# Two decoder layers on one core: expert stages regrouped, and the routing chain ahead of them rearranged

## What is computed

```
g_prob = softmax(xf @ wg + bg);  g_idx = argmax(g_prob)
e_sel  = (xf @ we + be) of the 8 experts of that group
top_v, top_i = top_k(e_sel, 2)                 # two experts per token
weights = g_w * softmax(top_v)
h = silu(xs @ w_gate[e]) * (xs @ w_up[e])      # 1024 -> 512, twice
y = (h @ w_down[e]) * weights                  # 512 -> 1024
x = x + sum of a token's two results
```

## Time and profile before

| | |
|---|---|
| median of 3 runs | 2049.12 us (2048.31 to 2049.97) |
| the profiled execution | 2047.72 us, its span 2046.0 us |
| PE busy | 1912.6 us, 93% of the span |
| DVE, ACT, POOL busy | 779.7, 536.8, 98.4 us |
| read from HBM | 486.44 MB |
| PE L976 (gate and up), L991 (down) | 22% and 11% of the chain that ended last |
| PE L946 (gathers), L968 (mixes) | 6% each of that chain |

### The profile page before, as it was taken

How to read it: one execution, slowest core, us unless ns; L and a number is a source line. 1 busy time by engine, 2 the same in 40 slices (tenths; PEclk the granted TensorE clock), 3 DMA queues, 4 the chain that set the end, 5 groups by cost and what they waited for, 6 DMA issues and landing times.

```text
span 2046.0 us, 22955 instructions
## 1 busy us (share of the span) xinstructions
PE 1912.6 (93%) x9568; PEld 1214.2 (59%) x9568; DVE 779.7 (38%) x1144; ACT 536.8 (26%) x968; POOL 98.4 (5%) x122
## 2 busy tenths in 40 slices
PE   6999999897999999999799969989879999999997
PEld 5875778674444444443588869967664444444443
DVE  4466564535222223222433363455352232222222
ACT  3416352533111111110244332334341111111110
POOL 2200010000000000000100050000000000000000
PEclk8999999998999999999899989989989999999999
DMA  6220342134999999999424302323127999999996
GB/s 228 83 67 16 104 144 83 42 101 177 405 408 406 409 405 410 407 404 415 165 93 144 99 12 96 105 102 103 37 90 299 411 406 407 405 412 410 402 410 258
DMA packets 99930, 490.09 MB, mean 240 GB/s; under 512 B 7760, under 2 KB 16016, under 8 KB 50544
## 3 DMA queue, kind: packets, MB, share of 16 engines
q1 hardware_dynamic: 96928, 478.18, 59.7%
q0 software_dynamic: 2320, 8.29, 1.2%
q10 hardware_dynamic: 576, 2.10, 0.3%
HBM read 486.44 MB, written 2.10 MB: 239 GB/s over the span
## 4 chain that ended last, share of the span: by engine, by line
PE 84%; DVE 6%; ACT 5%; issue 3%; POOL 1%; DMA 0%; DVEq 0%; ACTq 0%; POOLq 0%
PE ps L623 25%; PE ps L976 22%; PE ps L991 11%; PE ps L946 6%; PE ps L968 6%; PE ps L620 6%; PE ps L903 1%; PE ps L790 1%; PE ps L884 1%; ACT hT L1485 1%; DVE wl L510 1%; PE ps L636 1%; ACT wh L501 1%; DVE nat L1620 1%; DVE xnl L2105 1%
## 5 line engine op out<-in xcount | busy, mean ns | idle before, releaser
L976 PE MATMUL ps<-ring,xg 128*64 128x512 f32 x1536 | 346.3, 596 | 2.8 <-issue 2.5
L510 DVE TENSOR_TENSOR wl<-ring,wh 128x512 fp32r<-128x512 f32 x280 | 192.0, 695 | 388.4 <-ACT wh L501 387.4
L501 ACT ACTIVATE wh<-ring 128x512 fp32r<-128x512 f32 x280 | 174.2, 629 | 428.4 <-PE ps L623 350.7
L2097 DVE TENSOR_TENSOR x<-ps,x 128x1024 f32<-128x1024 f32 x128 | 150.6, 1219 | 334.7 <-PE ps L968 334.7
L623 PE MATMUL ps<-wh,ah 128*128 128x512 f32 x544 | 217.7, 400 | 7.5 <-DVE wl L510 3.1
L976 PEld LDWEIGHTS ps<-ring,xg 128*64 128x64 f32 x1536 | 105.2, 137 | 201.2 <-issue 196.9
L623 PE MATMUL ps<-wl,ah 128*128 128x512 f32 x544 | 214.9, 395 | 0.0
L623 PE MATMUL ps<-wh,al 128*128 128x512 f32 x544 | 214.8, 395 | 0.0
L991 PE MATMUL ps<-ring,hT 128*64 128x512 f32 x768 | 173.6, 601 | 4.7 <-ACT hT L1485 1.4
L1509 ACT ACTIVATE xg<-ps,grow 128x256 f32<-128x256 f32 x128 | 53.4, 470 | 350.0 <-PE ps L946 327.7
L2093 DVE TENSOR_TENSOR yl<-ps,yh 128x1024 fp32r<-128x1024 f32 x32 | 39.2, 1224 | 234.4 <-ACT yh L1488 234.4
(11 more groups left out here) (300 smaller groups left out, 2601.4 us busy)
## 6 DMA issues: line engine op xcount, KB each, us to landing
ring<-in_moe_w_gate SPq DMA_DIRECT2D x96, 1024.0 KB, 9.2
ring<-in_moe_w_up SPq DMA_DIRECT2D x96, 1024.0 KB, 8.3
ring<-in_moe_w_down SPq DMA_DIRECT2D x96, 1024.0 KB, 8.4
slot<-in_moe_w_up SPq DMA_DIRECT2D x32, 1024.0 KB, 8.8
slot<-in_moe_w_gate SPq DMA_DIRECT2D x32, 1024.0 KB, 9.2
slot<-in_moe_w_down SPq DMA_DIRECT2D x32, 1024.0 KB, 9.0
ring<-in_x_wkv SPq DMA_DIRECT2D x16, 1024.0 KB, 5.1
ring<-in_c_w_in SPq DMA_DIRECT2D x16, 1024.0 KB, 5.2
```

The source lines that it names most:

```text
L501: act.activation(wh[:, t % STAGE, :], ring[:, unit % RING, 512 * s:512 * (s + 1)], ACT.Copy).then_inc(wh_ready, 1)
L510: dve.tensor_tensor(wl[:, t % STAGE, :], ring[:, unit % RING, 512 * s:512 * (s + 1)], wh[:, t % STAGE, :].bitcast(F32), ALU.subtract).then ...
L976: mm = pe.matmul(ps[p * SLOTS:(p + 1) * SLOTS, bank, :], xg[:, b % 2, k, r * P + p * SLOTS:r * P + (p + 1) * SLOTS], w(p)[:, k % 4, :], st ...
L2097: return dve.tensor_tensor(x[:, m, :], ps[:, bank:bank + 2, :].rearrange("p a n -> p (a n)"), x[:, m, :], ALU.add)
```

## The change

Pair q on PE becomes: gate 0, gate 1, up 0, up 1; gather; mixes 0 and 1 of pair q-1; gather; mixes 2 and 3; hidden transposes, slot weights, slot transposes; down 0, down 1. With the next pair's gate and up that makes six weight stages in a row. The slot transposes move to bank 5. DVE forms the hidden rows ahead of the four adds; results are split in two halves of 512 columns by ACT and DVE. Ahead of the experts, the token split is done in halves of the columns: the first half beside the last dense product, the second behind `lgT`; two transposes are placed ahead of a product; `all_taken` moves behind the first gate stage; `most_slots` goes ahead of the second `oh`; and matmuls whose results nobody reads run where PE would wait (17 ahead of the ranks, 7 ahead of the first gathers).

```diff
-GATE, UP, TURN, Y, GATHER, MIX, SEL = 0, 1, 2, 3, 5, 6, 6
+GATE, UP, TURN, Y, GATHER, MIX, SEL = 0, 1, 2, 3, 5, 6, 5
...
+            def idle_products(bank, n):
+
+                for _ in range(n):
+                    pe.matmul(ps[:, bank, :].rearrange("p (a n) -> p a n", n=P), identr[:, :],
+                              identr[:, :].unsqueeze(1).to_broadcast([P, TM, P]), start=True, stop=True)
...
                 products(0, 0, (0, 4))
-                products(0, 1, (0, 4))
                 for m in range(3):
                     x_turn(l, 1, m)
+                products(0, 1, (0, 4))
...
                 b = begin(("rank", l, 0))
+                idle_products(b + 2, 17)
                 pe.wait_ge(S["cnt_ready"], l + 1)
...
                     if bank == GATHER:
                         after(pe, S["xg_ready"], 4 * (b0 + b) + block)
+                        if b and block % 2 == 0:
+                            pe.wait_ge(S["selT_ready"], q0 + 2 * b + block // 2 - 1)
...
                 def first_gathers():
 
+                    idle_products(GATHER, 7)
                     pe.wait_ge(S["oh_ready"], b0 + 1)
...
                 def do_mix(q, m, bank):
                     if m == 0:
-                        pe.wait_ge(S["y_split"], q0 + q + 1)
-                        pe.wait_ge(S["selT_ready"], q0 + min(q + 2, PAIRS))
-                    if m >= 2:
-                        pe.wait_ge(S["y_added"], 4 * (q0 + q) + m - 1)
-                    mix(q, m, bank).then_inc(S["mixed"], 1)
...
+                        pe.wait_ge(S["selT_ready"], q0 + q + 1)
+                        after(pe, S["y_added"], 4 * (q0 + q))
+                        for half in range(2):
+                            pe.wait_ge(S["y_split"], 2 * (q0 + q) + half + 1)
+                            mm = mix_half(q, 0, bank, half)
+                    else:
+                        if m >= 2:
+                            pe.wait_ge(S["y_added"], 4 * (q0 + q) + m - 1)
+                        mm = mix(q, m, bank)
+                    mm.then_inc(S["mixed"], 1)
...
                     do_hidden(q, GATE, 0)
-                    if q:
-                        do_mix(q - 1, 0, MIX)
-                        do_mix(q - 1, 1, Y)
-                    else:
+                    if q == 0:
+                        all_taken(pe, ("nmix", l + 1, 0))
                         do_gather(0, 3, Y + 1)
...
                     do_hidden(q, UP, 0)
-                    if q:
-                        do_mix(q - 1, 2, MIX)
-                        do_mix(q - 1, 3, Y)
...
                         do_gather(b + 1, 2 * (q % 2), GATHER)
+                    if q:
+                        do_mix(q - 1, 0, MIX)
+                        do_mix(q - 1, 1, Y)
+                    if more:
+                        do_gather(b + 1, 2 * (q % 2) + 1, GATHER)
+                    if q:
+                        do_mix(q - 1, 2, MIX)
+                        do_mix(q - 1, 3, Y)
                     pe.wait_ge(S["h_ready"], q0 + q + 1)
...
                     do_down(q, 1)
-                    if more:
-                        do_gather(b + 1, 2 * (q % 2) + 1, GATHER)
...
                 for m in range(TM):
-                    high(1, m)
+                    xn_high(0, m)
+                for m in range(3):
+                    high(1, m)
+                square(1, 0)
+                high(1, 3)
+                for m in range(1, TM):
                     square(1, m)
...
-                xn_his((0, 1))
                 b = round_done(act, ("route", l, 0)) + 3
                 act.activation(lgT[:, :], ps[0:2 * ROUTES, b, :], ACT.Copy).then_inc(took(("route", l, 0)), 1)
-                xn_his((2, 3))
+                for m in range(TM):
+                    xn_high(1, m)
...
                 def pair(q):
...
+                    hide(q)
                     if q:
                         for m in range(TM):
                             do_add(q - 1, m, Y if m % 2 else MIX)
...
                 columns(0)
-                for m in range(1, TM):
-                    xn_lo(l, m)
+                for m in range(TM):
+                    xn_lo(l, 1, m)
                 slot_table(l)
+                most_slots(l)
                 columns(1)
-                most_slots(l)
```

More of the change, by code:

```diff
@@ L962, in slots_T, with mix_half @@
                 return mm
+            def mix_half(q, m, bank, half):
+                for i, a in enumerate((yh, yl)):
+                    mm = pe.matmul(ps[:, bank + half, :], selT[:, q % 2, m * P:(m + 1) * P],
+                                   a[:, 512 * half:512 * (half + 1)], start=(i == 0), stop=(i == 1))
+                return mm
             def mix(q, m, bank):
                 for half in range(2):
-                    for i, a in enumerate((yh, yl)):
-                        mm = pe.matmul(ps[:, bank + half, :], selT[:, q % 2, m * P:(m + 1) * P],
-                                       a[:, 512 * half:512 * (half + 1)], start=(i == 0), stop=(i == 1))
+                    mm = mix_half(q, m, bank, half)
                 return mm
@@ L1123, in experts @@
                 pair(PAIRS - 1)
[L1124 to L1127, removed]
+                do_mix(PAIRS - 1, 0, MIX)
+                do_mix(PAIRS - 1, 1, Y)
+                do_mix(PAIRS - 1, 2, MIX)
+                do_mix(PAIRS - 1, 3, Y)
                 pe.wait_ge(S["y_added"], TM * PAIRS * (l + 1))
@@ L1488, in results_hi, with result_hi @@
                 return act.activation(yh[:, :], ps[:, Y:Y + 2, :].rearrange("p a n -> p (a n)"), ACT.Copy)
+            def result_hi(half):
+                return act.activation(yh[:, 512 * half:512 * (half + 1)], ps[:, Y + half, :], ACT.Copy)
             def experts(l):
                 q0, b0 = PAIRS * l, BATCHES * l
-                def xn_his(tiles):
-                    for m in tiles:
-                        act.activation(as_row(xnh[:, m, :]), by_row(x[:, m, :]), ACT.Copy).then_inc(S["xn_hi"], 1)
-                xn_his((0, 1))
                 b = round_done(act, ("route", l, 0)) + 3
                 act.activation(lgT[:, :], ps[0:2 * ROUTES, b, :], ACT.Copy).then_inc(took(("route", l, 0)), 1)
-                xn_his((2, 3))
+                for m in range(TM):
+                    xn_high(1, m)
                 act.wait_ge(S["g_sub"], l + 1)
@@ L1527, in pair @@
                         gathered(b + 1, 2 * (q % 2), GATHER)
+                        gathered(b + 1, 2 * (q % 2) + 1, GATHER)
                     act.wait_ge(S["hT_done"], q0 + q + 1)
@@ L1532, in pair @@
                     after(act, S["mixed"], 4 * (q0 + q))
-                    results_hi().then_inc(S["yh_ready"], 1)
-                    if more:
-                        gathered(b + 1, 2 * (q % 2) + 1, GATHER)
+                    for half in range(2):
+                        result_hi(half).then_inc(S["yh_ready"], 1)
                 gathered(0, 0, GATHER)
@@ L1974, in cross @@
                     low(0, m)
+                for m in range(2):
+                    xn_lo(l, 0, m)
                 b = round_done(dve, ("xo", l, 1))
@@ L2094, in results_lo, with result_lo @@
                                          ALU.subtract)
+            def result_lo(half):
+                part = slice(512 * half, 512 * (half + 1))
+                return dve.tensor_tensor(yl[:, part], ps[:, Y + half, :], yh[:, part].bitcast(F32), ALU.subtract)
             def add(m, bank):
@@ L2098, in add, with xn_lo @@
                                          ALU.add)
[L2100 to L2105, removed]
+            def xn_lo(l, c, m):
+                n = 2 * TM * l + TM * c + m
+                dve.wait_ge(S["xn_hi"], n + 1)
+                dve.tensor_tensor(half_row(xnl[:, m, :], c), half_by_row(x[:, m, :], c), half_row(xnh[:, m, :], c).bitcast(F32),
                                   ALU.subtract).then_inc(S["xn_lo"], 1)
@@ L2165, in experts @@
                 pair(PAIRS - 1)
-                for m, bank in enumerate((MIX, Y, GATE, MIX)):
-                    do_add(PAIRS - 1, m, bank)
+                for m in range(TM):
+                    do_add(PAIRS - 1, m, Y if m % 2 else MIX)
                 with dve.If(n > SLOTS):
@@ L2204, in _ @@
                 cross(l)
-                xn_lo(l, 0)
+                for m in range(2, TM):
+                    xn_lo(l, 0, m)
                 route(l)
```

38 lines of the change are left out of this document (20 added, 18 removed).

## The result

The changed kernel takes 2030.17 us (median of 4 runs, 2024.31 to 2031.18) against 2049.55 for the kernel before (4 runs beside it). The ratio is 0.9899, 95% interval 0.9878 to 0.9919: faster by 1.0%. I had predicted 2010, and 2000 to 2026. The sign was right, the size about twice too large, and the time lies outside the range. The profiled execution took 2031.18 us, its span is 2029.4.

A forecast was written before the change was run, and what follows sets the result against it. PE was taken to set the 30.95 us period, with loads close behind. Per layer 6.3 - 0.5 + 10.4 + 2.0 + 0.7 = 18.9 us, twice 37.8, off 2047.72 gave 2009.9, predicted as 2010; range 2000 to 2026.

The forecast's parts named there:

- What bounded the kernel before: Experts' pairs: PE sets the 30.95 us period, with the load limit only 0.8 to 1.5 us below.
- The steady pair on PE: Steady expert pairs: six stages 20.73 plus a group of 9.42 give 30.15 us, 0.80 less, 10.4 us a layer.
- The loads: Expert weight loads: engines keep up at 418 GB/s or more; up 1 lands at about 16, needed at 17.2.
- the loads set it: Rival, steady pairs: loads below 418 GB/s set the period, 9 to 20 us less gain, 2019 to 2029; chance 0.20.
- The last pairs: Pairs 14 and 15, without gathers: 26.9 us each, gains of 1.1 and 0.9, together 2.0 a layer.
- Pair 0: First pair of a layer, without mixes: some 0.5 us longer, as its second gather waits for ACT's copy.
- Ahead of the experts: Routing to first expert stage: 3.0 from earlier logits, 2.1 from DVE's halves, 1.2 from PE's wait; 6.3 us a layer.
- The clock: Rival, ahead of the experts: half clock delays the gathers, 2.5 us a layer lost, 2015; chance 0.08.
- The ends of the layers: Layer's end: halved results start the mixes 0.9 earlier, the four adds lengthen by 0.2; 0.7 us gained.
- Slower: Rival, steady pairs: up 1 starves, slower when its landing takes over 11.8 us; 53 us slower at 13.8; chance 0.03.
- adds hidden: Rival, steady pairs: mixes and adds overlap better, loads bind at 29.6 to 29.9 us, 1996 to 2004; chance 0.10.
- does nothing: Rival, steady pairs: broken runs cost the same inside a group, the period stays, only the ends gain, 2031; chance 0.01.

The follow-up runs named there:

- e2: Kernel before the change, with the experts' weight loads cut to 14% fewer bytes: 2048.99 us, ratio 1.0002.
- e3: Changed kernel with the low half of every mix left out, 1.8 us less PE work a pair, loads unchanged: 2014.94 us.
- e1: Changed kernel with the experts' weight loads cut to 14% fewer bytes: 2009.95 us, ratio 0.9814 to the kernel before.
- e8: Changed kernel with 33 unread products ahead of the ranks in place of 17, and 5 ahead of the gathers in place of 7: 2029.87 us.
- e10: Kernel before with only the part of the change ahead of the experts, its pairs left as they were: 2037.85 us, ratio 0.9955.
- e12: Changed kernel with mixes 0 and 1 between gate 1 and up 0, and 33 and 5 unread products for 17 and 7: 2023.94 us, ratio 0.9879.

## Why the prediction was wrong, point by point

By the two profiled executions 16.5 us were gained in place of 37.8. The missing 21.3 are 7.3 in the thirteen periods of each layer, 8.3 from the fifteenth pair's first stage to the last down stage's end, 1.1 in pair 0, 2.5 ahead of the experts and 4.0 outside the change, less 1.9 more than forecast at the ends.

**What bounded the kernel before:** right. e2 shows that PE alone set 30.95.

**The steady pair on PE:** right, 30.09 for 30.15. The adds end last, by 0.29 us. This step alone would have given 0.86 a period.

**The loads: the step that failed.** I had asked whether the mean rate sufficed (418 GB/s) and whether up 1's load, "there at about 16", came before 17.2. It came at 17.4 in the pair shown (559.52 - 542.13), 10.3 after its permission, with a use that stands 10.3 after it. The room was even less than that: PE starts 0.14 behind the landing, and a stage behind a wait takes 3.65 in place of 3.43, so a landing later than about 9.9 costs. My 16, that is 9.1 after the permission, had been worked out from a mean rate, as if all of a load arrived at once. In the steady pairs the load's first steps came at 8.3 to 8.9 and its last at 9.6 to 11.2, and wherever the last was later than 9.9 the period was that landing plus 20.15.

```profile
547.10:559.50 12.40, 12.40 (x58) 4.65 (x54) 1.29 (x2) 1.77 (x3) 0.00 (x0) 1.00 0.98 400
```

The engines were not idle meanwhile: between 547.1 and 559.5 they moved 400 x 12.4 = 4.96 MB, of which the four up loads are 4.19. The queue had not run dry either, as I had thought it nearly would: when up 0's loads were issued (545.82), two gate loads were still to land, the second from 547.47 to 549.34. From the steps' times I estimate that some 0.3 MB of the other 0.8 belonged to this load, ahead in the queue, and some 0.5 MB to the down loads behind, moved while the last share of up 1 lagged. The cost in the steady pairs was 9.2 us of stretch, 7.5 us against the forecast.

The rival "the loads set it" had the right cause, and said 2019 to 2029 at 0.20. It had the wrong rule: loads that always queue reach 420 (e3), and what binds is the distance of 10.3 us against the landing of a load's last share. And I ended the range at 2026, inside it.

**The last pairs: a second failure of the same step.** I took PE's 26.9 for both, and in e1 they are nearly that (26.95 to 27.6). But a pair's loads take 30.0, so without gathers PE outruns them. The last two intervals, down 0 to down 0, were 27.7 and 29.8 in the first layer, 27.0 and 31.1 in the second, where before they were 30.1 and 27.7. Against e1 that is 7.1 us for both layers, and against 26.9 each time it is 7.9. It needed no measurement: 26.9 stood beside 29.9 in the prediction.

**Pair 0:** 1.0 us a layer longer, from the first stage to the next pair's, where I had allowed 0.5.

**Ahead of the experts:** 4.8 and 5.3 us in place of 6.3. The logits came 3.0 earlier, as forecast (from the routing's start to L2034 9.3, before 12.3), DVE's halves took 4.13 (4.4 forecast), and PE no longer stood before the first stage for DVE. The clock took 1.0 to 1.6 back; I had named that, but set it at nothing in the sum. Where it held, in e8, the way was 25.8, that is 6.4 and 6.2 less than before: the rest of this step was right.

**The ends of the layers:** 0.6 for the first, 0.7 forecast. At the end of the kernel 2.7, but 1.7 of it comes from the clock and not from the change: in the profiled execution of the kernel before, the last two down stages took 8.8 us, the granted clock being 0.81 from 2023 to 2032; in e10, whose pairs are the same, they took 7.1.

**Outside the change:** the first 456 us are the same instructions, and were 2.9 us longer in this execution; the dense part of the second layer was another 1.0 longer. Over the kernels profiled here the routing of the first layer began between 454.8 and 460.4 us. That is the spread of single executions, and a reason not to read one of them to the us.

**Slower, adds hidden, does nothing:** none happened. The mechanism of the slower rival, up 1 starving, is the one that acted, in a mild form. Its landing was 11.2 at the longest in the steady pairs. I had given its landings a threshold of 11.8 us for a loss and had not priced the range from 10.3 to 11.8.

## What to carry to other kernels

When a change makes one engine's period shorter, set the new period beside that of every stream that fed the old one. For each buffer, set the time from its permission to its use beside the time at which the last share of its load lands, with its spread, and not beside the mean rate: a slack of nothing costs part of each late landing, even where both rates suffice. Do this apart for the stretches at the ends, where work is left out and the balance is another. Waiting time spent on products nobody reads should be filled whole: 17 products left up to 3.4 us of it and the clock fell on every way, 33 filled it and the clock held on five of six.

## What the runs showed of the hardware

Two paces of 30.09 (PE) and 30.0 (loads) gave 30.46 together. In a full queue 1 MB loads landed in order, their first shares 2.48 us apart, but a load's last share came 1.0 to 2.6 us behind its first in the changed kernel, and one share that fell 1.4 us behind (at 541.90) held up the loads after it too. Halving the loads from 1 MB to 512 KB cost 3% of the rate (408 against 420 GB/s, with the engines busy throughout). The level traffic of the kernel before, share 1.01 at 409 GB/s, looked like a limit and was none: with 14% fewer bytes nothing changed (e2). The granted clock fell in a pause of 3.4 us in the first layer and came back during the gathers. It also fell in shorter pauses: behind one of 1.14 us in the changed kernel's second layer and in e12's first, while in e8 it held through the same one.
